# Conditioning pairs of a hybrid transformer block: plain fp32 products with stationary weights in place of split weights and turned rows

## The reference, cut to what matters

```
shift, scale, gate = jnp.split(jax.nn.silu(c) @ w_ada + b_ada, 3, axis=-1)
shift_c, scale_c, gate_c = jnp.split(jax.nn.silu(c_ctx) @ w_ada + b_ada, 3, axis=-1)
h = rms_norm(x, norm_g) * (1.0 + scale[:, None]) + shift[:, None]
h_c = rms_norm(ctx, norm_g) * (1.0 + scale_c) + shift_c
... = jnp.split(h @ w_in, IN_SPLITS, axis=-1)
```

## Time and profile before

| | us |
|---|---|
| median of 3 runs | 1923.2 |
| lowest and highest | 1922.72, 1926.9 |
| profiled execution, whole | 1927.93 |
| its span | 1926.1 |
| TensorE products busy | 1799.3 |
| VectorE, ScalarE, GpSimd busy | 1127.7, 971.5, 669.2 |

### The profile page before, as it was taken

How to read it: one execution, slowest core, us unless ns; L and a number is a source line. 1 busy time by engine, 2 the same in 40 slices (tenths; PEclk the granted TensorE clock), 3 DMA queues, 4 the chain that set the end, 5 groups by cost and what they waited for, 6 DMA issues and landing times. The chain is left out here.

```text
span 1926.1 us, 27717 instructions
## 1 busy us (share of the span) xinstructions
PE 1799.3 (93%) x11060; PEld 1497.2 (78%) x11060; DVE 1127.7 (59%) x1610; ACT 971.5 (50%) x1297; POOL 669.2 (35%) x490
## 2 busy tenths in 40 slices
PE   6789996899999999999999978999798999999999
PEld 5678886898888888888788857878696787777777
DVE  5556495459667656553234255749759866465343
ACT  6657523336445455553653156753337564555661
POOL 0011421537743434453153000144346544433150
PEclk9899998999999999999999999999799999999999
DMA  7123224422221122233244213324222221212352
GB/s 300 34 77 110 72 72 146 133 67 59 95 77 44 55 72 75 82 104 116 89 129 163 96 54 96 98 78 121 78 67 66 77 66 55 72 50 91 106 186 87
DMA packets 76414, 178.86 MB, mean 93 GB/s; under 512 B 6464, under 2 KB 29312, under 8 KB 76160
## 3 DMA queue, kind: packets, MB, share of 16 engines
q1 hardware_dynamic: 34272, 122.46, 20.6%
q10 hardware_dynamic: 42016, 54.63, 8.3%
HBM read 156.00 MB, written 21.07 MB: 92 GB/s over the span
## 5 line engine op out<-in xcount | busy, mean ns | idle before, releaser
L506 PE MATMUL banks<-hH,wHs 128*128 128x512 f32 x1984 | 599.0, 364 | 46.9 <-DVE hL L474 20.5
L506 PE MATMUL banks<-hH,wLs 128*128 128x512 f32 x1984 | 582.8, 355 | 0.0
L506 PE MATMUL banks<-hL,wHs 128*128 128x512 f32 x1984 | 581.1, 355 | 0.0
L1973 POOL TENSOR_TENSOR wLs<-raw,wHs 128x512 fp32r<-128x512 f32 x272 | 410.8, 1536 | 465.2 <-ACT wHs L872 465.2
L506 PEld LDWEIGHTS banks<-hH,wHs 128*128 128x128 f32 x1984 | 327.0, 191 | 123.6 <-issue 26.1
L506 PEld LDWEIGHTS banks<-hL,wHs 128*128 128x128 f32 x1984 | 324.8, 191 | 55.5 <-issue 2.2
L506 PEld LDWEIGHTS banks<-hH,wLs 128*128 128x128 f32 x1984 | 324.6, 191 | 54.7
L872 ACT ACTIVATE wHs<-raw 128x1024 fp32r<-128x1024 f32 x210 | 219.7, 1053 | 219.4 <-DMA raw<-wstream 219.2
L1529 DVE SCALAR_TENSOR_TENSOR acc<-padc,vecs,acc 128x783 f32<-128x783 f32 (+1 forms) x240 | 294.6, 1281 | 0.0
L861 ACT ACT_TABLE_LOAD x180 | 230.9, 1283 | 30.2 <-issue 13.0
L906 ACT ACTIVATE Pa<-banks,stat 128x768 f32<-128x768 f32 (+1 forms) x80 | 64.6, 813 | 144.0 <-DVE stat L1467 144.0
(11 more groups left out here) (242 smaller groups left out, 2330.8 us busy)
## 6 DMA issues: line engine op xcount, KB each, us to landing
raw<-wstream SPq DMA_DIRECT2D x210, 512.0 KB, 3.6
araw<-wstream SPq DMA_DIRECT2D x16, 512.0 KB, 12.6
E<-g_rows ACTq DMA_DIRECT2D x16, 384.0 KB, 7.0
egb<-eg_rows ACTq DMA_DIRECT2D x20, 256.0 KB, 4.2
inb<-intra_rows ACTq DMA_DIRECT2D x20, 256.0 KB, 4.5
parked_logits<-sg ACTq DMA_DIRECT2D x13, 384.0 KB, 4.1
xs<-xT SPq DMA_DIRECT2D x8, 384.0 KB, 11.4
intra_rows<-E ACTq DMA_DIRECT2D x8, 384.0 KB, 3.1
```

The costliest lines, as they stand in the source:

```text
L506: last = pe.matmul(out[:, a:b], w, m[:, kt, a:b], start=(kt == 0 and j == 0), stop=(kt == kts - 1 and j == 2))
L1973: ins = pool.tensor_tensor(wL[w % RING][:, o:o + 512], raw[w % RING][:, o:o + 512], wH[w % RING][:, o:o + 512].bitcast(F32), ALU.subtract)
```

## The change

All 24 pairs are done in plain fp32 the other way round: the unit's 128x128 blocks are stationary, straight from `raw` or `araw`, and the moving operand is `cs32`, the two vectors' columns. No pair's weights are rounded or subtracted any more, `csx`, `awH`, `awL`, `adar` and `ada_turn` are gone, and results stand on the partitions where they are used. For the first eight pairs VectorE adds the bias (`first_col`), for the others ScalarE, in two steps.

In the opening the eight pairs come in the order 0, 4, 1, 5, 2, 6, 3, 7 of outputs (`FIRST_PAIR`), so that shift and scale of two tiles are known after each second pair. x is loaded in three pieces, after pairs 0, 1 and 2, and its sums stand there too; `nh` is cut into four items between the later pairs. Of the ring's units only the first is prepared in the opening, just ahead of the last two tiles. No engine calls `ahead` or `low` at a pair.

```diff
+FIRST_TILES = ((0, 1, 2), (3, 4, 5), (6, 7), (), (), (), (), ())
+FIRST_PAIR = (0, 4, 1, 5, 2, 6, 3, 7)
...
-    for t in range(KT):
-        out += [("ada", 0, t), ("nsum", 0, t)]
+    for v, t in enumerate(FIRST_TILES[:4]):
+        out += [("ada", 0, v)] + [("nsum", 0, i) for i in t]
+    out += [("ada", 0, 4), ("nh", 0, 0), ("ada", 0, 5), ("nh", 0, 1), ("nh", 0, 2), ("ada", 0, 6), ("ada", 0, 7), ("nh", 0, 3)]
...
-                    out = product(pe, pair, 2 * P)
-                    pe.wait_ge(*done("csL"))
+                    out = product(pe, pair, 4)
+                    pe.wait_ge(*done("cs32"))
                     if first_ada(l, m):
...
+                        pe.wait_ge(*done("araw", 2 * m + 1))
+                        w = [araw[:, 2 * m + j, :] for j in range(2)]
+                    else:
+                        for u in units_of(it):
+                            pe.wait_ge(*done("raw", u))
+                        w = [raw[WIDX[u] % RING] for u in units_of(it)]
+                    for j in range(2):
+                        for kt in range(KT):
+                            last = pe.matmul(out[:, 2 * j:2 * j + 2], w[j][:, kt * P:(kt + 1) * P],
+                                             cs32[:, kt, :], start=(kt == 0), stop=(kt == KT - 1))
...
+            for v, tiles in enumerate(FIRST_TILES):
+                for m in (2 * v, 2 * v + 1):
+                    sp.dma_start(araw[:, m, :], wstream[m]).then_inc(*tick("ada_raw%d" % v, "araw", m, by=16))
...
+                if tiles:
+                    x = slice(tiles[0], tiles[-1] + 1)
+                    sp.dma_start(xs[:, x, :], xT[:, x, :]).then_inc(*tick("x_tiles%d" % v, "xt", tiles[0], by=16))
...
+                    done_hi[0] += 1
+                    if v[0] == "ada":
+                        continue
                     act.wait_ge(*done("raw", v))
...
-                    if l == 0 and m == 6:
-                        ahead(UNITS[0])
-                    for u in units_of(it):
-                        ahead(u, ada_lead(l, m))
+                    if first_ada(l, m):
+                        continue
                     pair = ("adap", l, m)
                     act.wait_ge(*done("pe", pair))
...
+                    for j in range(2):
+                        act.activation(ada[:, l, 2 * m + j, :], place[pair][:, 2 * j:2 * j + 2], ACT.Identity,
+                                       bias=vecs[:, l, V_BADA + 2 * m + j:V_BADA + 2 * m + j + 1]).then_inc(
...
                 elif k == "nh":
-                    for t in range(KT):
+                    if l == 0 and it[2] == 3:
+                        ahead(UNITS[0], 1)
+                    for t in (2 * it[2], 2 * it[2] + 1):
...
                 elif k == "nh":
-                    dve.wait_ge(*done("gs", l))
+                    i = it[2]
+                    if l == 0 and i == 3:
+                        low(UNITS[0], 1)
+                    dve.wait_ge(*done("gs", l, KT - 1 if l else 2 * i + 1))
...
             for it in ITEMS:
                 stage[0], k, l = it[0], it[0], it[1]
-                if k == "ada":
-                    for u in units_of(it):
-                        ahead(u, ada_lead(l, it[2]))
-                    if l == 0 and it[2] == 6:
-                        ahead(UNITS[0])
-                elif k == "gb":
+                if k == "gb":
```

More of the change, by code:

```diff
@@ L101 @@
 LEAF_PARKS = (3, 6)
+FIRST_TILES = ((0, 1, 2), (3, 4, 5), (6, 7), (), (), (), (), ())
+FIRST_PAIR = (0, 4, 1, 5, 2, 6, 3, 7)
 def schedule():
     out = []
-    for t in range(KT):
-        out += [("ada", 0, t), ("nsum", 0, t)]
+    for v, t in enumerate(FIRST_TILES[:4]):
+        out += [("ada", 0, v)] + [("nsum", 0, i) for i in t]
+    out += [("ada", 0, 4), ("nh", 0, 0), ("ada", 0, 5), ("nh", 0, 1), ("nh", 0, 2), ("ada", 0, 6), ("ada", 0, 7), ("nh", 0, 3)]
     for l in range(DEPTH):
-        out += [("nh", l), ("gb", l)]
+        out += ([("nh", l, i) for i in range(4)] if l else []) + [("gb", l)]
         for h in range(NT):
@@ L209, in low_on_vector @@
 def low_on_vector(u):
-    return u[0] in ("gb", "dk", "dv", "dq", "cz", "branch2", "branch0", "wout") or u[0] == "ada" and u[1] == 0
-FIRST = [("ada", 0, m) for m in range(2 * KT)]
+    return u[0] in ("gb", "dk", "dv", "dq", "cz", "branch2", "branch0", "wout")
+FIRST = [("ada", 0, 2 * m + j) for m in FIRST_PAIR for j in range(2)]
 ITEMS = schedule()
@@ L241, in build @@
         names += ["park_out0", "park_out1", "leaf_out0", "leaf_out1"] + ["park_in%d" % i for i in range(4)]
-        names += ["ada_raw%d" % i for i in range(KT)]
+        names += ["ada_raw%d" % i for i in range(KT)] + ["x_tiles%d" % i for i in range(3)]
         names += ["g_out", "eg_out", "e_in0", "e_in1", "i_out0", "i_out1"]
@@ L567, in values @@
                 last.then_inc(*tick("pe", "pe", key))
[L569 to L583, removed]
             pe.wait_ge(*done("ones"))
@@ L1451, in scales, with first_col @@
-            def scales(l):
-                dve.wait_ge(*done("ada", l, KT - 1))
-                dve.scalar_tensor_tensor(gs[:, l, :, :], ada[:, l, 8:16, :], 1.0,
-                                         bc(vecs[:, l, V_NG:V_NG + KT], 2), ALU.add,
-                                         ALU.mult).then_inc(*tick("dve", "gs", l))
+            def first_col(v):
+                pair, m = ("adap", 0, v), FIRST_PAIR[v]
+                dve.wait_ge(*done("pe", pair))
+                dve.tensor_tensor(ada[:, 0, 2 * m:2 * m + 2, :], place[pair][:, 0:4].rearrange("p (u c) -> p u c", u=2),
+                                  bc(vecs[:, 0, V_BADA + 2 * m:V_BADA + 2 * m + 2], 2), ALU.add).then_inc(*tick_read("dve", pair))
+                got[("ada", 0, v)] = got[("read", pair, 0)]
+                if v % 2:
+                    scales(0, slice(v - 1, v + 1), v)
@@ L1458, in maxes, with scales @@
+            def scales(l, tiles=slice(0, KT), last=KT - 1):
+                dve.wait_ge(*done("ada", l, last))
+                dve.scalar_tensor_tensor(gs[:, l, tiles, :], ada[:, l, 8 + tiles.start:8 + tiles.stop, :], 1.0,
+                                         bc(vecs[:, l, V_NG + tiles.start:V_NG + tiles.stop], 2), ALU.add,
+                                         ALU.mult).then_inc(*tick("dve", "gs", l, last))
             def maxes(l, h, qt):
@@ L1509, in _ @@
             last_gm = [None, None]
-            first_lo = [0]
             conv_done = [0]
```

129 lines of the change are left out of this document (22 added, 107 removed).

## The result

The changed kernel took 1974.6 us in the median (1969.7 to 1982.1) against 1923.4: the ratio is 1.0276, with a 95% interval of 1.0243 to 1.0308. It is slower by 51 us, where 7 were forecast; the direction was right, the size far outside the range of 1904 to 1957.

A forecast was written before the change was run, and what follows sets the result against it. TensorE, busy for 93% of the span, was taken as the bound. Opening 9.8 gained, stretch 0, dout 8.5, late pairs 4.3 and clock 3.4 lost: 6.4 us slower, 1930 us, range 1904 to 1957.

The forecast's parts named there:

- The price of a pair: Each new pair on TensorE: 32 records at 86 ns, 2.8 us at full clock, with bounds of 40 and 112 ns.
- the upper row: Upper bound on a pair's record distance: plain fp32 products 112 ns apart, giving 3.6 us a pair.
- At half clock it doubles: Pairs at half clock were forecast at 150 ns a record, 4.7 us each, with 7 us as upper end.
- 9.8 us of gain: Opening: gb's result read at 63.7 instead of 73.5 us, so 9.8 us gained.
- Whether pairs hold the clock: All pairs: a run of two-column pairs was taken neither to raise nor to hold the granted clock.
- two of ten late pairs: Late part: two of ten pairs followed by a stretch at half speed, 1.7 us each, 3.4 us lost.
- The stretch from 305 us: Early pairs among block products, 305 to 350 us: sum of -1 to +1, put at 0.
- the rival: Case of loads at 107 ns, doubled at half clock: its term for the stretch was 11 us lost.
- dout: Start of item dout: TensorE waits 6.5 us for GpSimd, some 2 us more at half clock, 8.5 lost.
- The late pairs' preparation: Late part: roundings and subtractions taken off ScalarE and GpSimd, about 3 us a unit, hidden beside TensorE, give nothing.
- Long loads, 107 ns and twice that at half clock: All pairs at 3.5 and 6.9 us: 39 us slower, 1962, chance 0.15; if clock holds, 1930, chance 0.08.
- the late terms: Ten late pairs: 4.3 us lost for the pairs themselves and 3.4 lost to the clock.

The follow-up runs named there:

- e4: Changed kernel with 128 moving columns in each pair and dz prepared ahead: 1915.1 us, ratio 0.9954 to the kernel before.
- e5: Changed kernel with 128 moving columns, dz prepared ahead, and the opening's order changed so scaling and unit gb start earlier: 1909.2 us, ratio 0.9932.
- e3: Changed kernel, still two moving columns, with the first two units of dout (dz 0 and 1) rounded and subtracted ahead: 1970.2 us, ratio 1.0228.
- e11: 128-column kernel with dz ahead, plus the ten late pairs' rounding and GpSimd subtraction put back though their products use neither: 1919.9 us, ratio 0.9987.
- e12: Fastest kernel (new opening order, 128 columns, late pairs in old form), with VectorE instead of GpSimd writing the late pairs' low parts: 1901.9 us, ratio 0.9885.

## Why the prediction was wrong, point by point

**The price of a pair was taken from the wrong end.** I had bounds of 40 and 112 ns and took 86, from the starts of two loads after a pause (100 ns) less what transposing loads needed. At full clock the records stand 109 ns apart with 2 and 32 columns, 110 with 64 and 112 with 128. So the upper row, which I had set aside because "the load hides beside the columns", held the price within 3 ns. A clean late pair is 3.49 us instead of 2.8. The old one with its turn is 2.30 in the mean of the ten, so the new one costs 1.2 more instead of 0.43: 12 us for ten instead of 4.3, and 12.7 in e4 with 128 columns. The Trainium skill's 107 ns for a load of 128 columns ("TensorE: Matmul & The Clock Gate", LDWEIGHTS), which I had given only as a rival, agrees with these 109.

**At half clock it doubles.** I took 150 ns, from 170 against 100 in one place; the pair at 6.42 shows 213, as do the rows at 0.50. (The place of the 170, 11.71 us, reads 1.00 in the clock's column like the pair at 6.42, so it was no sure row for the lower level.) So a pair took up to 6.8 us instead of 4.7, and pair 4 ended at 48.4 and not at 36.7. Of these 11.7 us the five pairs make 8 and the eight column sums 3.9: they took 16.1 us instead of 12.2, since I had them slow behind pair 0 alone, and twelve products behind pair 0 took 6.97 us and twelve behind pair 1 6.42, against 3.9 each time in e4. Scaling, pair 7 and gb followed. 9.8 us of gain became 7.4 of loss. The reordering itself was good: with the clock up, e4 is 11.2 us ahead of the kernel before at the product of L638 (90.35 us before) and e5 17.4.

**Whether pairs hold the clock** was called rightly, from the earlier trace rows: with two columns they don't raise or hold it. But I let that act only where the clock was low anyway, with a fall behind two of ten late pairs, 3.4 us. It fell at eight. By e4, in which it doesn't fall, the clock cost 19 us of the late part's 24.9 (24.9 less e4's own 6.1, between the same two products), the largest single term of the loss. A pair of two-column products between dense units, 3.5 us long, was enough for it at eight places of ten; I had treated it as a short pause.

**The stretch from 305 us** was put at 0 and lost 10.1. The row of events was as foreseen (pair 9 starts at 316.00 when its weights land, without VectorE's wait), but six pairs of up to 6.9 us stood where I had 4.7, together some 10 us more. The wait for `egb` at the scan's start gave back 1.8 us (5.3 before, 3.5 after), where I had 1. In the rival I had 11 for the stretch.

**dout** was right in every part: 6.5 us of hole forecast and 6.34 found, GpSimd's subtraction behind its squares as its end, 8.5 in all and 8.8 found, and e3 and e4 close it.

**The late pairs' preparation** was said to give nothing, since TensorE never waits there. It did wait, twice 1.7 us for a VectorE that GpSimd had slowed, and the late part of e4 shows 6.6 us given back (12.7 for the pairs against 6.1 lost). The 3.2 of them beyond the two waits are in smaller pieces that I didn't follow. I had read the list of waits for its large entries only, and had not asked whom GpSimd slows.

**The choice among the rivals.** "Long loads, 107 ns and twice that at half clock" described what happened; its 1962 fell 12 us short, mainly in the late part (18 for pairs and clock instead of 24.9) and in the opening (2 instead of 6.4). It had 0.15. Its strongest evidence was in my own rows: 112 ns at 128 columns, and the sum was most sensitive to just this number, 24 pairs times 32 records.

**The direction** came out right, but not by the sum as it stood: the opening, its largest term, had the wrong sign. It was right by dout and by the sign of the late terms.

## What to carry to other kernels

A product with few moving columns and a full plain fp32 load costs what 128 columns cost, so widen it before you judge it: the columns are all but free in time (3.57 us a pair instead of 3.49), and here they kept TensorE's clock up. Read a trace's busy share and its granted clock together, since TensorE was 100% busy at half speed from 40 to 60 us. And where VectorE and GpSimd work at the same time, look at the duration of the same instruction in a place where one rests: work that is hidden on one engine may be paid for on the other.

## What the runs showed of the hardware

- Plain fp32 products with 128x128 weights: 109 ns from record to record with 2 and 32 moving columns, 110 with 64, 112 with 128, two records a product; 213 to 215 ns at half speed.
- Granted clock over the opening's row of pairs, TensorE recorded as busy for 95% or more: 0.50 with 2 and with 32 moving columns, 1.00 with 64 and 128. Among block products (busy for 83 to 93%): 0.50 with 2, 32 and 64 columns, 0.89 with 128.
- Beside a subtraction on GpSimd (2.54 us alone, 3.32 together), two convolution steps of VectorE took 2.98 instead of 1.97 us and a scaling of 128x768 took 1.18 instead of 0.62 (before and e11 against e4); with ScalarE's rounding there and GpSimd at rest they took 1.97 and 0.62 (e12).
- The column of the granted clock read 1.00 until 22 us of the changed kernel's trace, while its first pair's records stood 213 ns apart.
